# Projections of two blocks computed by seven half-size products instead of eight

## What is computed

```python
# first block
p_lat = (_layer_norm(h_x) * (1.0 + sc_l[:, None]) + sh_l[:, None]) @ w_in[l]
p_ctx = (_layer_norm(h_ctx) * (1.0 + sc_c) + sh_c) @ w_in[l]
pv_l, u_l, fh_l, g_l = _split_proj(p_lat)     # u: RWKV, fh: HGRN (q, i, z forwards, z backwards)
u_l = _shift3(u_l, rwkv_shift[l])
# second block, in each of two layers
h = _rmsnorm(x, g_mix)
proj = h @ w_in                               # 1024 x 7244
(qa, ka, va, qb, kb, vb, fl, qc, kc, vc, qi, ki, wi, gl) = jnp.split(proj, COL_SPLITS, axis=-1)
br_a = _stick_breaking_attention(heads(qa, 8), heads(ka, 8), heads(va, 8))
br_b = _forgetting_attention(heads(qb, 8), heads(kb, 8), heads(vb, 8), log_f)
# br_c: attention over the 64 best keys of each token, found from qi, ki, wi
x = x + y @ w_out
x = x + jnp.square(jax.nn.relu(_rmsnorm(x, g_mlp) @ w_up)) @ w_down
```

## Time and profile before

| | us |
|---|---|
| median of three runs | 1642.99 |
| lowest, highest of the three | 1633.76, 1645.26 |
| profiled execution, its time | 1639.52 |
| profiled execution, its span (first to last instruction) | 1637.7 |
| mean granted PE clock, share of full speed | 0.984 |
| busy: PE, DVE, ACT, POOL | 1573.9, 655.5, 347.1, 19.3 |

### The profile page before, as it was taken

The page is one execution under the profiler, slowest core; times in us unless marked ns, Lnnn a source line. Parts: engine busy times, 40 slices in busy tenths (PEclk is TensorE's granted clock), DMA queues, the critical chain, the costliest instruction groups (busy, mean ns, idle before and its releaser), DMA issues.

```text
span 1637.7 us, 29142 instructions
## 1 busy us (share of the span) xinstructions
PE 1573.9 (96%) x12883; PEld 1287.3 (79%) x12883; DVE 655.5 (40%) x1292; ACT 347.1 (21%) x731; POOL 19.3 (1%) x33
## 2 busy tenths in 40 slices
PE   7999999799799899999999999999999999999998
PEld 2544458688688687778788999998777778899998
DVE  2431034555652414223421766521413343176643
ACT  1201132533432302033400121001103340012100
POOL 3000001000000000000000000000000000000000
PEclk9999999899899899999999999999999999999999
DMA  9222240000011524422244444463442224444451
GB/s 350 101 67 87 77 155 3 3 2 18 2 41 67 131 103 154 154 103 103 103 154 154 141 169 155 170 166 112 146 154 104 103 108 149 154 155 155 162 189 49
DMA packets 110894, 191.49 MB, mean 117 GB/s; under 512 B 20889, under 2 KB 27297, under 8 KB 110641
## 3 DMA queue, kind: packets, MB, share of 16 engines
q1 hardware_dynamic: 109776, 188.29, 33.2%
q0 software_dynamic: 960, 1.33, 0.2%
q10 hardware_dynamic: 32, 0.01, 0.0%
HBM read 188.57 MB, written 1.05 MB: 116 GB/s over the span
## 4 chain that ended last, share of the span: by engine, by line
PE 88%; issue 3%; DVE 2%; ACT 2%; PEld 1%; DMA 1%; DVEq 1%; PEldq 1%; ACTq 1%; SPq 0%
PE psum L1255 21%; PE psum L1109 19%; PE psum L1194 10%; PE psum L831 6%; PE psum L1365 5%; PE psum L1117 4%; PE psum L756 4%; PE psum L1300 2%; PE psum L992 2%; PEld psum L1365 1%; PE psum L1380 1%; PE psum L1180 1%; PE psum L1223 1%; DMA arena<-in_x 1%; PE psum L1334 1%
## 5 line engine op out<-in xcount | busy, mean ns | idle before, releaser
L1255 PEld LDWEIGHTS psum<-arena 128*128 128x128 f32 x3136 | 350.5, 192 | 0.1
L1255 PE MATMUL psum<-arena 128*128 128x128 f32 x3136 | 350.5, 275 | 0.0
L1109 PE MATMUL psum<-arena 128*128 128x256 f32 x1440 | 314.2, 379 | 0.0
L1109 PEld LDWEIGHTS psum<-arena 128*128 128x128 f32 x1440 | 272.4, 189 | 40.3 <-issue 1.3
L1784 ACT ACTIVATE arena<-psum 128x512 f32<-128x512 f32 (+6 forms) x246 | 125.8, 517 | 709.2 <-PE psum L1255 176.7
L1194 PE MATMUL psum<-arena 128*128 128x256 f32 x768 | 176.5, 382 | 0.0
L1194 PEld LDWEIGHTS psum<-arena 128*128 128x128 f32 x768 | 141.9, 190 | 26.4 <-issue 5.3
L1365 PE MATMUL psum<-arena 128*128 128x512 f32 (+1 forms) x368 | 139.6, 538 | 1.1 <-issue 1.0
L1365 PEld LDWEIGHTS psum<-arena 128*128 128x128 f32 x368 | 69.3, 190 | 71.5 <-issue 69.0
L831 PE MATMUL psum<-arena 64*64 64x64 f32 x3072 | 96.6, 219 | 2.1 <-issue 2.0
L831 PEld LDWEIGHTS psum<-arena 64*64 64x64 f32 x3072 | 92.6, 134 | 7.5 <-issue 5.3
(11 more groups left out here) (342 smaller groups left out, 1468.2 us busy)
## 6 DMA issues: line engine op xcount, KB each, us to landing
arena<-in_w_in SPq DMA_DIRECT2D x33, 2048.0 KB, 7.8
arena<-in_w_up SPq DMA_DIRECT2D x16, 2048.0 KB, 8.0
arena<-in_w_down SPq DMA_DIRECT2D x16, 2048.0 KB, 7.9
arena<-in_w_out SPq DMA_DIRECT2D x6, 2048.0 KB, 8.0
arena<-in_w_branch SPq DMA_DIRECT2D x6, 2048.0 KB, 7.8
arena<-in_mod_w SPq DMA_DIRECT2D x5, 2048.0 KB, 14.0
arena<-in_w_in SPq DMA_DIRECT2D x3, 1024.0 KB, 6.7
arena<-in_w_in SPq DMA_DIRECT2D x12, 256.0 KB, 4.8
```

What stands on the lines that cost most here:

```text
L1109: mm = pe.matmul(b[:, i * T:(i + 1) * T], w[:, k, c:c + P], src[:, k, :], start=k == 0, stop=k == ks - 1)
L1255: mm = pe.matmul(b[:, n * P:(n + 1) * P], left[:, k, n * P:(n + 1) * P], right[:, k, :], start=first and n == 0 and k == 0, stop=last and ...
```

## The change

Three chunks of the first block (5, 8 and 9: u4 to u7, fh4 to fh7, fh8 to fh11) and the six head chunks of both layers go over to seven products. POOL makes their sums of weights and, for the first block, the sums of tokens; DVE makes the token sums of the layers (`token_sums1`, four operations of 128x512 behind `normed`) and the sums of the results. For u4 to u7 these go to SBUF (`u_raw`) and are shifted from there after the last product. DVE multiplies with cos and sin for all five rotated parts and then adds, with two fences in place of ten. The eight search rounds are divided into 2, 3 and 3 between the result sums. The scale 0.125 of qb moves into the mask of B.

```diff
-TAIL = "TTETETTTTTTTTETETETEHTETEHTHTHTETHTEH"
+TAIL = "TTETETTTTTTTTTETETETEHTETEHTHTHTETHEH"
...
+PRODUCTS_FIRST = (1, 6, 7, 5, 2, 3, 4)
+PRODUCTS_IN_STEPS = (PRODUCTS_FIRST[0:2], PRODUCTS_FIRST[2:4], PRODUCTS_FIRST[4:6], PRODUCTS_FIRST[6:7])
 GROUPS = {
-    "T": [[(f"fh{t}", "A", 1)] for t in range(12)]
+    "T": [[(f"fh{t}", "A", 1)] for t in range(4)]
+         + [[(f"f{c}_{m}", "D", 1) for m in ms] for c in (1, 2) for ms in PRODUCTS_IN_STEPS]
...
+              + [(f"u_{m}", "D") for m in PRODUCTS_FIRST] + [(f"u{t}", "D") for t in range(8, 11)])
...
+HEAD_PARTS = ("qa", "ka", "va", "qb", "kb", "vb")
+HEAD_PRODUCTS = (1, 6, 7, 5, 2, 3, 4)
...
+        p += [(f"{x}_{m}", "A" if m == 1 else "D", 1) for m in HEAD_PRODUCTS]
...
+CHUNK_ENDS = (["qc1", "qi", "fl"] + [f"{x}_4" for x in HEAD_PARTS] + [f"gl{2 * n + 1}" for n in range(6)]
...
+        u_raw = hz[:, 0:4]
+        fh_out = arena[:, hi_at + 512:hi_at + 9 * 512].rearrange("p (t n) -> p t n", n=512)
...
+        FIRST_BY_SEVEN = (5, 8, 9)
...
+                xp.wait_all(gp)
+                x11, x12, x21, x22 = token_halves(xt, T)
+                t1, t2, t3, t4 = [tok_first[:, n] for n in range(4)]
+                gp.tensor_tensor(t1, x12, x11, ALU.subtract)
+                gp.drain()
+                gp.tensor_tensor(t2, x22, t1, ALU.subtract)
+                gp.tensor_tensor(t3, x22, x12, ALU.subtract)
+                gp.drain()
+                gp.tensor_tensor(t4, t2, x21, ALU.subtract)
+                gp.drain().then_inc(sem("first_tokens_summed"), 1)
+                for i, n in enumerate(FIRST_BY_SEVEN):
+                    gp.wait_ge(s_slot[SLOT[n]], landed(n))
+                    s1, s2, s4 = [first_sums[i % 2][:, x] for x in range(3)]
+                    w11, w21, w12, w22 = quarters(ring[:, SLOT[n]])
+                    gp.tensor_tensor(s1, w21, w22, ALU.add)
+                    gp.drain()
+                    gp.tensor_tensor(s2, s1, w11, ALU.subtract)
+                    gp.tensor_tensor(w21, w11, w21, ALU.subtract)
+                    gp.drain().then_inc(sem("first_weights_summed"), 1)
+                    gp.tensor_tensor(s4, w12, s2, ALU.subtract)
+                    gp.drain().then_inc(sem("first_weights_summed"), 1)
                 gp.wait_ge(s_used, 15)
...
+                for l in range(LAYERS):
+                    if l:
+                        ly.wait_emptied(gp, "br23", l - 1)
+                    for i in range(len(HEAD_PARTS)):
+                        n = len(FIRST) + 3 + i
+                        gp.wait_ge(s_slot[SLOT[n]], l * SLOT_PER_LAYER[SLOT[n]] + landed(n))
+                        if i >= 2:
+                            ly.wait_filled(gp, f"{HEAD_PARTS[i - 2]}_4", l)
+                        s1, s2, s4 = [head_sums[:, i % 2, x] for x in range(3)]
...
+            def head_product(b, x, i, w, m):
+
+                s1, s2, s4 = [head_sums[:, i % 2, y] for y in range(3)]
+                w11, w21, w12, w22 = quarters(w)
+                x11, x12, x21, x22 = token_halves(ht)
+                t1, t2, t3, t4 = [tok1[:, y] for y in range(4)]
+                left, right = {1: (w11, x11), 6: (s2, t2), 5: (s1, t1), 7: (w21, t3), 2: (w12, x21), 3: (s4, x22), 4: (w22, t4)}[m]
+                if m == 6:
+                    pe.wait_ge(sem("token_sums1"), l + 1)
+                    pe.wait_ge(sem("head_weights_summed"), 2 * (len(HEAD_PARTS) * l + i) + 1)
+                if m == 3:
+                    pe.wait_ge(sem("head_weights_summed"), 2 * (len(HEAD_PARTS) * l + i) + 2)
+                if x[0] == "v":
+                    for k in range(half):
+                        mm = pe.matmul(b[:, 0:T], right[:, k, :], left[:, k, :], start=k == 0, stop=k == half - 1)
+                    return mm
+                for n in range(2):
+                    for k in range(half):
+                        mm = pe.matmul(b[:, n * P:(n + 1) * P], left[:, k, n * P:(n + 1) * P], right[:, k, :], start=k == 0, stop=k == half - 1)
+                return mm
...
-                for n in range(2):
-                    if x[0] == "v":
-                        tokens(f"{x}{n}", w, 0, 512, n)
-                    else:
-                        tiles(f"{x}{n}", w, (2 * n * P, (2 * n + 1) * P))
+                for m in HEAD_PRODUCTS:
+                    head_product(take_bank(ly, f"{x}_{m}", l), x, i, w, m).then_inc(ly.filled, 1)
...
-                        ly.wait_emptied(pe, "vb1", l)
+                        pe.wait_ge(sem("heads_added"), len(HEAD_PARTS) * l + 5)
...
+                    if i == 1:
+                        pe.wait_ge(sem("heads_added"), len(HEAD_PARTS) * (l + 1))
...
+                def product(b, i, m):
+
+                    n = FIRST_BY_SEVEN[i]
+                    w = use_chunk(pe, n)
+                    s1, s2, s4 = [first_sums[i % 2][:, x] for x in range(3)]
+                    w11, w21, w12, w22 = quarters(w)
+                    x11, x12, x21, x22 = token_halves(xt, T)
+                    t1, t2, t3, t4 = [tok_first[:, x] for x in range(4)]
+                    left, right = {1: (w11, x11), 6: (s2, t2), 5: (s1, t1), 7: (w21, t3), 2: (w12, x21), 3: (s4, x22), 4: (w22, t4)}[m]
+                    if m == 6:
+                        pe.wait_ge(sem("first_tokens_summed"), 1)
+                        pe.wait_ge(sem("first_weights_summed"), 2 * i + 1)
+                    if m == 3:
+                        pe.wait_ge(sem("first_weights_summed"), 2 * i + 2)
+                    for n in range(2):
+                        for k in range(half):
+                            mm = pe.matmul(b[:, n * T:(n + 1) * T], left[:, k, n * P:(n + 1) * P], right[:, k, :], start=k == 0, stop=k == half - 1)
+                    return mm
...
+                    if chunk == 1:
+                        for m in PRODUCTS_FIRST:
+                            product(take_bank(setup, f"u_{m}"), 0, m).then_inc(setup.filled, 1)
+                        used()
+                        continue
...
-                    for t in range(12):
-                        if t % 4 == 0:
-                            w = use_chunk(pe, 7 + t // 4)
-                        project(take_bank(tl, f"fh{t}_0"), t, 7 + t // 4, w, t % 4 * P).then_inc(tl.filled, 1)
-                        if t % 4 == 3:
+                    w = use_chunk(pe, 7)
+                    for t in range(4):
+                        project(take_bank(tl, f"fh{t}_0"), t, 7, w, t * P).then_inc(tl.filled, 1)
+                        if t == 3:
                             used()
                         yield
+                    for c in (1, 2):
+                        for ms in PRODUCTS_IN_STEPS:
+                            for m in ms:
+                                product(take_bank(tl, f"f{c}_{m}_0"), c, m).then_inc(tl.filled, 1)
+                            if ms == PRODUCTS_IN_STEPS[-1]:
+                                used()
+                            yield
...
+                ly.wait_filled(act, f"{x}_1", l)
+                b = bank(ly, f"{x}_1", l)[:, 0:T]
+                emptied(ly, copy(head_quarters(x, dst)[0], b if x[0] == "v" else blocks_of(b)))
...
+                if j == 0:
+                    act.wait_ge(sem("fh_added"), d + 1)
...
+            def added(pool, group, out):
+
+                c11, c12 = [out[:, 0:2, s] for s in (slice(0, T), slice(T, 2 * T))]
+                c21, c22 = [out[:, 2:4, s] for s in (slice(0, T), slice(T, 2 * T))]
+
+                def p(m):
+                    pool.wait_filled(dve, group(m))
+                    return blocks_of(bank(pool, group(m)), T)
+
+                emptied(pool, dve.tensor_copy(c11, p(1)))
+                fence()
+                emptied(pool, dve.tensor_tensor(c12, p(6), c11, ALU.add))
+                fence()
+                emptied(pool, dve.tensor_tensor(c21, p(7), c12, ALU.add))
+                fence()
+                p5 = p(5)
+                dve.tensor_tensor(c22, p5, c21, ALU.add)
+                emptied(pool, dve.tensor_tensor(c12, p5, c12, ALU.add))
+                fence()
+                emptied(pool, dve.tensor_tensor(c11, p(2), c11, ALU.add))
+                emptied(pool, dve.tensor_tensor(c12, p(3), c12, ALU.add))
+                emptied(pool, dve.tensor_tensor(c21, c21, p(4), ALU.subtract))
...
+                for _ in range(7):
                     yield
+                added(tl, lambda m: f"f1_{m}_0", fh_out[:, 0:4])
+                done("fh_added")
+                for _ in range(4):
+                    yield
+                added(tl, lambda m: f"f2_{m}_0", fh_out[:, 4:8])
+                done("fh_added")
...
+            def head_added(x, dst):
+                c11, c12, c21, c22 = head_quarters(x, dst)
+
+                def p(m):
+                    ly.wait_filled(dve, f"{x}_{m}", l)
+                    b = bank(ly, f"{x}_{m}", l)[:, 0:T]
+                    return b if x[0] == "v" else blocks_of(b)
+
+                ly.wait_emptied(dve, f"{x}_1", l)
```

(41 more changed lines are left out.)

91 lines of the change are left out of this document (65 added, 26 removed).

## The result

The changed kernel takes 1619.18 us (median of 4 runs, 1617.27 to 1623.64) against 1639.59 us (4 runs, 1633.76 to 1645.26): ratio 0.9882, 95% interval 0.9854 to 0.9910. Beside its later variants on one chip it took 1622.73 us (6 runs) against 1639.43 (11 runs): 0.9893 (0.9871 to 0.9916). So it is faster by 1.1 to 1.2%, 17 to 20 us, where 1614 us and a gain of 26.8 us were forecast. The profiled execution took 1617.27 us, its span 1615.4 at a mean granted clock of 0.984: 22.3 us under that of before.

A forecast was written before the change was run, and what follows sets the result against it. PE bounds the kernel, its time following the columns streamed. 28.4 + 1.4 - 2 - 1 = 26.8 us off 1639.5 gives 1612.7; half the 3.5 us between median and profiled execution makes 1614, range 1604 to 1629.

The forecast's parts named there:

- Matmuls: PE in first stage and heads: time goes with columns; seven products save 10.0, 11.4 and 7.0 us, 28.4 in all.
- the wait at z0: Start of attention in each layer: PE's idle 0.69 us before z0 goes away, a gain of 1.4 us.
- POOL's price: Each of 64 two-input POOL sums of 128x1024 costs between 0.9 and 2.65 us; the upper end was taken.
- the recursion: Heads: POOL starts a chunk's sums once the chunk two before has ended; it breaks at 3.65 us an operation.
- case D: Slower or no gain: POOL sums stall the start and each layer, deciding from 4.26 us an operation; chance 0.05.
- The start: First stage, chunk 5: POOL's sums must be ready by 73.7 us; 2 us charged, between 0 and 5.
- rival A: POOL operations hold out DVE operations with two SBUF inputs, at the start and in each layer: 1621 us; chance 0.15.
- Heads and DVE: Heads: DVE's 6.4 to 8.0 us of work fits each 12.5 us chunk; at the scores 11 us of slack.
- B: In the heads `head_added` at twice 3.4 us starves PE's banks: 2 to 3 us in some four places, 1624; chance 0.07.
- Turns: First stage: one T turn less lies between H and E turns; 1 us charged, 0 to 2.
- Case C: First stage: E and H turns bound by ACT and DVE, so 6.7 us return as idle PE, 1620; chance 0.07.
- The signs: Right: forecast instruction counts and times, POOL at most 2.7 us, no z0 wait; wrong: PE waits, idle PE, lower clock.

The follow-up runs named there:

- the run with double work: The changed kernel with eight POOL operations a head chunk instead of four, three sums being repeated with the same result: 1676.43 us (one run).
- the other list of turns: The changed kernel with only the order of its first-stage turns changed: 1618.29 us, ratio 0.9877 to the kernel before.
- the heads alone: The changed kernel with the first stage's edits undone, so only the six head chunks of each layer use seven products: 1621.28 us, 0.9892 of before.
- The version with late angles and the new turns: The changed kernel with the angles moved behind DVE's fifth T turn and the turns reordered: 1609.90 us (0.9833 of before), again 1609.71 (0.9807).

## Why the prediction was right, point by point

**Matmuls.** 0.112 and 0.218 us an instruction gave 24.4 us a first chunk (24.46 measured), 12.5 a query or key chunk (12.59) and 12.2 a value chunk (12.37 and 12.27). With the wait at z0 gone, the heads give 18.9 us where 19.8 were forecast. The first stage gives 9.9 us wherever nothing stalls; forecast 10.0.

**POOL's price.** 2.35 us an operation, and 2.00 for s2 = s1 - w11 every time, inside the bounds 0.9 and 2.65 that came from one and three streams of a memset. Its sums for chunk 5 were ready at 69.4 (first pair) and PE never waited for POOL. By the page of the Trainium skill that the prediction named (GPSIMD Engine Reference, Performance versus the Vector engine) it would be an estimated 2.25; the rows say 2.35. Why s2 takes less stays open: t2 = x22 - t1 also reads the sum made just before it, and took 2.35. This step was right; the recursion with which case D was dismissed named the place of the waits in the run with double work, and too little of their size.

**The start: the step that failed.** I charged 2 us, between 0 and 5, and asked mainly when POOL would be ready. The wait was for DVE: 6.7 us, and 1.7 of clock behind it, 8.4 in all. This was rival A's mechanism. It had the place and the size of DVE's delay right (an end near 73; 73.4), and took PE's wait to be 4.4; PE was there at 68.5 already, since chunk 4 had begun 1.6 us earlier, and the bank came free half a us later. The wait of POOL for DVE of some 5 us, which A added, did not exist: POOL keeps its pace and DVE pays. I gave A 0.15 because `head_added` reads one operand from PSUM. But the operations at the start read only SBUF: 16 of them (A counts 14), six tiny and ten at full width. Of the ten three have two inputs; six are TENSOR_SCALAR, of which I hadn't asked whether they are held, and those that met POOL were, even by writes alone. A's "a DVE operation with two SBUF inputs" names only a part of what was held.

**Heads and DVE.** The second half of A happened too, without a cost. From the timeline of DVE in the changed kernel:

```profile
640.79 4.45 DVE L2524 TENSOR_SCALAR arena<-arena 128x128 f32<-128x128 f32 x2 [2.19 <-ACTq L1902]
645.32 4.49 DVE L2526 SCALAR_TENSOR_TENSOR arena<-arena 128x128 f32<-128x128 f32 x6
...
650.36 0.42 DVE L2477 TENSOR_TENSOR arena<-psum,arena 128x256 f32<-128x256 f32 x1
```

The nine score operations take 9.6 us instead of 3.6; four operations of POOL take 9.4. va_6's bank is free at 650.8, and PE wants it for the third product of qb, at 651.79 + 2 x 1.79 = 655.4: 4.6 us are left of the 11 forecast. Where the work was given time, being held cost nothing. The searches and `head_added` (0.42 us an operation, as forecast) weren't late either, so B did not happen. The searches read and write SBUF only and weren't held at all:

```profile
652.10 2.36 POOL L799 TENSOR_TENSOR arena<-arena 128x1024 f32<-128x1024 f32 x1 [4.49 <-PE psum L1201]
```

```profile
653.50 0.62 DVE L2534 MAX8 arena<-arena 128x8 f32<-128x128 f32 x2 [0.18 <-issue]
```

Two MAX8 take 0.62 us in the middle of one of POOL's operations, as without POOL.

**Turns.** 1 us charged (0 to 2), 2.6 measured, and up to 4.4 more where the clock fell behind the wait. I had counted the T turns that stand between H turns and not looked at what ACT has to do between two E turns: two table loads of 1.28 us around a gate for which it must also wait. Case C named the right stretch for a loss but the wrong reason (ACT and DVE bound everywhere): the other list of turns took the loss away with the same work.

**The sum.** With the measured terms: 18.9 + 9.9 - 8.4 - 2.6 = 17.8 us, and 4 us less where the clock falls behind the 2.2 us wait. The two comparisons of medians give 20.4 and 16.7, the heads alone 16.9. The pair of profiled executions gives 22.3: 4.5 more than its terms. Of these 1.6 lie ahead of chunk 4 and 2.7 between the S turns and layer 0, where nothing was changed; I take them for the scatter between executions (no run tests it). So two losses in the first stage, together 11 us and 8 larger than charged, ate its whole gain of 9.9, which was computed rightly. That the first measurement still lies only 5 us above 1614 is luck in part: the second, 1622.73, lies 9 above. Nor do the times decide between my sum and A's 1621; the trace does, and it shows A's mechanism at the start.

**The signs.** Those for "right" came: 336 instructions in 75.0 us, 896 in 100.7, 224 in 49.3, 64 operations of POOL (at most 2.74 us, a little over my 2.7), no wait for POOL, none at z0. Of those for "wrong" two came as well: more idle PE between 190 and 260 us (6.5 us for 3.7), and a granted clock under 1.00 (0.65) where it had been 1.00. The wait for DVE ahead of chunk 5 was on neither list.

The version with late angles and the new turns beats both kernels: 1609.7 us, 1.8 to 1.9% under before.

## What to carry to other kernels

Work on an idle engine is free only if it shares nothing with the one that feeds the bottleneck: before sums go to POOL, list what DVE does in the same us with its operands in SBUF, give each such operation of a kind that was held here (TENSOR_SCALAR, TENSOR_TENSOR, SCALAR_TENSOR_TENSOR, scan) the length of one POOL operation, and follow the delay to the next bank that PE wants. If that is too late, move the work that has no hurry (here the angles, needed 500 us later), not the start of POOL. Price a new wait of PE with the clock behind it, and read the order of turns for each engine, ACT's tables too, and not only for PE.

## What the runs showed of the hardware

- While POOL read and wrote SBUF, these DVE operations from SBUF to SBUF were held until one of POOL's ended and took 1.5 to 2.5 us, whatever their own size: TENSOR_SCALAR, TENSOR_TENSOR, SCALAR_TENSOR_TENSOR and TENSOR_TENSOR_SCAN. A TENSOR_SCALAR of 128x6 took 2.18 instead of 0.18, those of 128x256 up to 2.5 instead of 0.30 to 0.36; small ones that fell between two of POOL's took their 0.17. POOL lost little: mostly 2.35, once 2.48 in the first stage, 2.5 and 2.7 once each a layer.
- Not held, in the middle of one of POOL's: the CAST from int32 (0.28), a RECIPROCAL of 128x6 (0.19), MAX8 (0.62 for two) and MATCH_REPLACE8 (0.28 and 0.41), and the sums with one input in PSUM (0.42). The runs don't say why.
- Against a POOL operation that only writes, TENSOR_SCALAR was held (2.5 us each) and SCALAR_TENSOR_TENSOR with two SBUF inputs was not (0.93 for two).
- Behind gaps of 6.7, 5.8, 6.3, 4.1 and 3.65 us in PE's work the granted clock was low; behind one of 2.2 us in four executions of seven, at a price of up to 4.4 us. What decides it in the last case stays open: the changed kernel itself gave both, with the same wait at the same place.
